# Four column tiles of 32 tokens in place of one 128-token matmul in the up products of an expert loop

## What is computed

```
def block(args):
    tok, e = args
    xb = h[tok]
    return (jax.nn.silu(xb @ w1[e]) * (xb @ w3[e])) @ w2[e]
```

## Time and profile before

| What | Value |
|---|---|
| median of the two runs | 1882.64 us |
| the profiled execution, its own time | 1882.96 us |
| its span, first to last instruction | 1881.2 us |
| what lies around the span | 1.8 us |
| mean granted TensorE clock over the span | 0.909 |
| expert loop, from the first gather to the last product | about 1092 to 1822 us of the span |
| matmul records of the up products | 1024, 451.5 us busy |
| matmul records of the down products | 512, 227.9 us busy |

### The profile page before, as it was taken

One profiled execution on the slowest core, in us unless ns is written; L12 is line 12 of the kernel. 1 busy time (PEld: TensorE's weight loads), 2 busy tenths in 40 slices (PEclk: granted clock), 3 DMA queues, 4 the chain that ended last, 5 costly groups with the idle time before them and its releaser, 6 DMA issues. The chain is left out here.

```text
span 1881.2 us, 18060 instructions
## 1 busy us (share of the span) xinstructions
PE 1669.7 (89%) x6288; PEld 1015.7 (54%) x6288; DVE 536.6 (29%) x1113; ACT 393.2 (21%) x979; POOL 300.0 (16%) x244
## 2 busy tenths in 40 slices
PE   8999999996778999999997269999999999999950
PEld 7666666664655677777774134444444444444420
DVE  1344444201335444444452500000000000000008
ACT  1211111111212344444430001111111111111112
POOL 0000000000314343333340001111111111111105
PEclk8999999998557999999997579999999999999975
DMA  6143222312322122222100169999999999999935
GB/s 227 43 116 110 71 71 71 93 59 78 111 90 78 64 72 86 91 90 90 73 35 23 59 220 337 330 340 339 339 327 339 332 330 339 339 339 326 340 103 190
DMA packets 173764, 334.21 MB, mean 178 GB/s; under 512 B 37560, under 2 KB 67176, under 8 KB 172424
## 3 DMA queue, kind: packets, MB, share of 16 engines
q1 hardware_dynamic: 163048, 294.30, 44.9%
q0 software_dynamic: 9504, 34.61, 7.0%
q10 hardware_dynamic: 1152, 4.52, 0.6%
HBM read 281.33 MB, written 52.07 MB: 177 GB/s over the span
## 5 line engine op out<-in xcount | busy, mean ns | idle before, releaser
L1893 PE MATMUL bank<-sb_arena 128*128 128x512 f32 x1024 | 451.5, 594 | 3.6 <-ACT sb_arena L1938 2.5
L358 PE MATMUL bank<-sb_arena 128*128 128x368 f32 x1344 | 421.1, 476 | 6.6 <-DMA sb_arena<-xT 6.6
L358 PEld LDWEIGHTS bank<-sb_arena 128*128 128x128 f32 x1344 | 257.4, 192 | 168.2 <-DMA sb_arena<-w_conv 6.6
L1893 PEld LDWEIGHTS bank<-sb_arena 128*128 128x128 f32 x1024 | 192.5, 191 | 234.5 <-issue 229.9
L1909 PE MATMUL bank<-sb_arena 128*128 128x512 f32 x512 | 227.9, 598 | 8.1 <-DMA sb_arena<-w 8.1
L1992 DVE TENSOR_SCALAR sb_oidx<-sb_slot 128x1 int32 x32 | 4.9, 154 | 548.0 <-DMA d_acc<-sb_arena,sb_oidx 547.9
L1909 PEld LDWEIGHTS bank<-sb_arena 128*128 128x128 f32 x512 | 95.8, 192 | 117.2 <-issue 108.9
L1867 POOL DMA_INDIRECT d_acc<-sb_arena,sb_oidx x32 | 51.0, 1592 | 613.3 <-ACT sb_arena L1956 613.3
L829 PE MATMUL bank<-sb_arena 128*128 128x512 f32 (+1 forms) x288 | 134.2, 607 | 5.8 <-DVE sb_rlog L1384 5.0
L1938 ACT ACTIVATE sb_arena<-bank 128x512 f32<-128x512 f32 x66 | 35.8, 594 | 276.6 <-PE bank L1887 276.6
L1335 DVE TENSOR_TENSOR sb_arena<-sb_arena,bank 128x256 f32<-128x256 f32 (+1 forms) x102 | 41.4, 413 | 159.5 <-PE bank L752 103.1
(11 more groups left out here) (315 smaller groups left out, 1711.8 us busy)
## 6 DMA issues: line engine op xcount, KB each, us to landing
sb_arena<-w SPq DMA_DIRECT2D x192, 1024.0 KB, 7.9
sb_arena<-w_conv SPq DMA_DIRECT2D x28, 512.0 KB, 4.7
d_conv<-sb_arena SPq DMA_DIRECT2D x28, 512.0 KB, 3.2
sb_arena<-d_conv SPq DMA_DIRECT2D x8, 1792.0 KB, 7.4
sb_arena<-d_gam SPq DMA_DIRECT2D x8, 768.0 KB, 4.0
d_x<-sb_arena SPq DMA_DIRECT2D x9, 512.0 KB, 2.6
sb_arena<-xT ACTq DMA_DIRECT2D x8, 552.0 KB, 9.5
sb_arena<-w_out SPq DMA_DIRECT2D x8, 512.0 KB, 4.8
```

What stands on the lines that cost most here:

```text
L358: last = e.matmul(bank[3 * r + s][:, 0:TN], wring[n % NV][:, k, :], xT[:, k, TN * s:TN * s + TN], start=(k == 0), stop=(k == KT - 1))
L1893: mm = e.matmul(bank[bk][:], xgT[:, k, :], w[:, k, :], start=(k == 0), stop=(k == KT - 1))
```

## The change

Each up product is written as four column tiles. For each k, the 128 tokens are cut into four groups of 32; each group is a matmul of its own, with 32 columns of the stationary operand, the same 512 moving columns of the weights, and an output of 32 partitions x 512 (partitions j to j + 31 of the same bank). The semaphore is incremented by the last matmul alone, as before. Nothing else changes.

```
                 def up(b, w, bk, done, arrived):
                     e.wait_ge(S[arrived], 32 * (b + 1))
                     for k in range(KT):
-                        mm = e.matmul(bank[bk][:], xgT[:, k, :], w[:, k, :], start=(k == 0), stop=(k == KT - 1))
+                        for j in range(0, P, 32):
+                            mm = e.matmul(bank[bk][j:j + 32, :], xgT[:, k, j:j + 32], w[:, k, :], start=(k == 0), stop=(k == KT - 1))
                     mm.then_inc(S[done], 1)
```

## The result

The changed kernel takes 1901.17 us (median of two runs, 1900.25 to 1902.09) where the kernel before takes 1882.64: a ratio of 1.0104, 95% interval 1.0088 to 1.0121. It is slower by 18.5 us, 1.0%, and not by the 460 us that were forecast. That is the second rival almost to the number (1904 us).

What follows compares the result with a forecast made beforehand. TensorE was taken to set the pace, with DMA a hair behind. 1883 + 439 (up products, pairs of tiles overlapping) + 21 (changes of shape) = 2343 us; range 2300 to 3350, the sum's own range 2320 to 2460.

Steps and rivals of the forecast that it cites:

- second rival: Up products: all four tiles stream in parallel, each with its own queue; only shape changes cost, 1904 us; chance 0.13.
- What bounds the kernel: Expert loop: TensorE sets the pace, DMA a hair behind; longer up products go onto the span one for one.
- changes of shape: Into and out of each tiled up call: 0.17 us for each of 126 changes, +21 us, bounds 0 and 32.
- the slots: Up calls: matmuls start in program order, so only two tiles overlap; 32 slots of 0.429 us, 13.73 us a call.
- the term of +439 us: Up products: 6.86 us more per call over 64 calls, from pairs of tiles overlapping.
- first rival: Up products: float32 matmuls in different column tiles don't overlap; 3222 us; chance 0.30, shared with the low clock.
- The weight loads: Up products: four times as many loads, 0.11 us long, 0.03 us apart, hidden under matmuls; 0, upper bound 102 us.
- The clock: Expert loop: clock stays at 1.00; a rival had it at 0.50, about 3220 us, chance 0.30 shared with no overlap.
- The bound on a gain: Expert loop: DMA at 98% would allow a shrink of 2% at most, 14 us, even with faster up products.

Runs made afterwards that it cites:

- k_pairs: Changed kernel with the same up matmuls reordered, two of k per tile at a turn; 1904.30 us.
- k_inner: Changed kernel with k as the inner loop, so each tile's eight up matmuls stand together; 2885.02 us.
- k_quads: Changed kernel with the same up matmuls reordered, four of k per tile at a turn; 2459.68 us.
- same_tile: Changed kernel with all four matmuls of a k taking the same 32 tokens and writing the same column tile; 3216.03 us.
- order_whole: Kernel before with the transposes of hm moved behind the second up product, nothing tiled; ratio 1.0016, 1883.35 us.
- order_tiled: Kernel before with the hm transposes behind the second up product and both up products tiled; ratio 1.0065, 1894.89 us.
- one_tile: Changed kernel with three of the four column tiles left out, 1024 records of 32 columns remaining; 1894.55 us.
- half_early: half_k with GpSimd's gather of a block issued ahead of the scatter of the block before it; 1811.26 us.
- half_k: Kernel before with only the first four of the eight matmuls of each up product, weight loads whole; 1933.98 us.

## Why the prediction was wrong

**What bounds the kernel: right.** PE is busy for all of the stretch before and after, and what the changes of shape cost comes out on the span in full: 31 x 0.572 = 17.7 of 18.5 us.

**The step that failed: the slots.** "If matmuls start in program order, tile 1's first record can't start before tile 0's second has." It can, and so can those of tiles 2 and 3: in the changed kernel all 16 slots of a call hold four starts, 7 ns apart, so a second record that waits for its tile's first holds no other tile back. A call has 16 slots and not 32, and the term of +439 us is 0 (by the busy times, 455.5 against 451.5 us, with part of the changes of shape in it). The prediction named the condition for this, "each tile has its own queue", as its second rival, and gave it 0.13.

Two steps are to be kept apart. The changed kernel alone shows only that records don't start in program order. Whole matmuls could still do so: for each k its four matmuls stand in four tiles, and none has to pass another. k_pairs rules that out too: each tile's second matmul waits there while the next tiles' first ones, which stand behind it in the program, start; in k_inner and k_quads exactly one waiting matmul is passed.

The rule of the Trainium skill in "TensorE: Matmul & The Clock Gate", Part 3, splits in two here: tiles of different column groups do run together, the starts being 7 ns apart where the page has about 4; that starts are strictly in program order fits the changed kernel if it is taken for whole matmuls, and is not what k_pairs, k_inner and k_quads show.

The argument against the rival was empty: that starts are "evenly spaced, with none ahead of its turn" described a trace in which no two neighbouring matmuls use different column tiles, and there is nothing to pass. Rows in which a mechanism had no chance to act carry no weight against it. The same holds for the first rival: its price was right (same_tile takes 3216 us where it had 3222), but no row spoke for it.

**The changes of shape: right in kind, close in size.** 0.17 us were taken for each, 0.143 measured, 18 us instead of 21. With +439 at 0, this term is the whole loss. The gaps on PEld are at the forecast places, 0.17 us on the way in, near the 0.2 forecast, but 0.84 on the way out, against 0.30 within the stream, and the runs order_whole and order_tiled show that the price hangs on the change itself. The Trainium skill's drain at a change of tiling mode ("TensorEngine Tiling (Array Packing)", Key Properties) agrees with that.

**The weight loads: right.** 110 ns each, as estimated, hidden under the matmuls, four of them to a slot and not two; up to eight within 0.18 us in k_pairs. Their distance was put at 0.03 us and is 7 ns.

**The clock: right.** 1.00 in the loop, with a quarter of the columns in use as well (one_tile).

**The bound on a gain: wrong.** DMA at 98% was to allow the loop to shrink "by 2% at most": half_early moves the same 334 MB at a higher rate in the loop and takes 1811 us. With half the up products' work gone, the kernel was first held by the ring through GpSimd's queue, which the prediction didn't see. What stands next behind TensorE in the kernel before, at full clock, is open: the ring by the sum above at about 20.6 us a block, or the weight loads, with which half_early's median is 20.4 at a mean clock of 0.94. Both are 6 to 7% below 21.9 and not 2%. The bound changed nothing in this forecast, since the change takes no work away, but the reasoning was unsound.

## What to carry to other kernels

Column tiles of one float32 product run side by side if the program goes round the tiles with at most two matmuls per tile at a turn; longer turns lose the overlap (16 slots became 36 with turns of four and 52 with turns of eight; turns of three were not run). Tiling a product that already fills 128 columns gains nothing, since a record costs its 512 moving columns whatever its width (1024 records of 32 columns are busy for 452.6 us, 1024 of 128 columns for 451.5), and each change between array shapes costs 0.14 us here, so tiled products belong next to each other. Before a cheaper product is counted as a gain, look for the ring that doesn't contain it: here less work on TensorE made the kernel slower, until the gather was issued ahead of the scatter.

## What the runs showed of the hardware that was not expected

- A float32 matmul of 128x32 starts ahead of one that stands before it in the program, if the two use different column tiles: one waiting matmul per tile is passed, a second one holds the others back (k_pairs, k_inner, k_quads).
- Four float32 tiles start within 0.02 us and stream 512 columns in the time of one, 0.429 us a record, at full clock.
- A change between 128x128 and column tiles costs 0.14 us, with two tiles as with four (periods of 22.513 and 22.487 against 21.915 us, four changes a block).
- A mean DMA share of 0.98 at 335 GB/s stands against 1.04 at 370 GB/s in half_early, which moves the same bytes in another order: the share is no measure of what is left.
- With 6.3 us of idle time in each block the granted clock fell to 0.50 ahead of the transposes (half_k): a down product took 8.4 us where it takes 6.9 in the kernel before. Taking work off an engine can so make the rest of its work slower.
